# The low part of the normalised rows moved by 64 bytes in a two-part transformer kernel

## The chip, the cores and the metric

The kernel runs on one core of one Trainium2 chip. The metric is device time in microseconds (us) of one execution; lower is better. The engines are PE (TensorE; "PEld" are its weight loads), DVE (VectorE), ACT (ScalarE), POOL (GpSimd) and SP (SyncE), each with its own queue of instructions. A core has one SBUF of 128 partitions, in which all operands of the products lie.

## The reference

Two transformer parts run one after the other on a sequence of 256 rows of 1024 float32 numbers. The first has two layers, the second two. Cut to what the change touches:

```
h = rms_norm(x, g_mix[l]);  proj = h @ w_in[l]            # 1024 x 10052, split over four branches
x = x + merged @ w_merge[l]
h2 = rms_norm(x, g_ffn[l])
x = x + (silu(causal_dwconv(h2 @ w_ffn_gate[l])) * (h2 @ w_ffn_up[l])) @ w_ffn_down[l]
...
h = rmsnorm(x, norm_mix[layer]);  proj = h @ w_in          # second part: compressed and dilated attention
x = x + mix @ w_out
x = x + swiglu(rmsnorm(x, norm_ffn[layer]), ffn_w_up[layer], ffn_w_down[layer])
```

All weights are float32, and the result is to be close to a float32 computation.

## The kernel before

**Split products.** TensorE works in fp32r, a shortened float32. So every float32 operand is split into a high part (the value rounded to fp32r) and a low part (value minus high part), and each product is made in three passes by `three_passes`: high x high (L469), high x low (L470), low x high (L471). In the trace, a name pair as `psum<-hT,whi` gives the streamed operand first and then the one that is loaded as a block of weights.

**Weights.** They come in 277 units of up to 128x2048 numbers (8192 bytes a partition). SP loads a unit into one of three slots of `raw`; ACT makes the high part in one of four slots of `whi` (L437); DVE, or POOL for some, makes the low part in one of three slots of `wlo` (L445); PE multiplies. SP may refill a slot of `raw` once its low part is made.

**Rows.** The normalised rows, turned so that the 1024 features lie on the partitions, are `hT[0]` (high) and `hT[1]` (low), each of 8 x 256 numbers a partition. In the column form (`columns_product`, L486, and others) a block of the weights is loaded and the rows are streamed, 256 columns at a time: pass L470 streams `hT[1]` past a block of `whi`. In the row form (`psum<-whi,hT`) a block of the rows is loaded and the weights are streamed, 256, 512 or 68 columns at a time: pass L471 has a block of `hT[1]` loaded. `hT` is written by `whole_high` (L615, ACT) and `whole_low` (L623, DVE), and at the end of each mixing part by L1440 and L1710, L2161 and L2354, L2581 and L2632. The first units after each normalisation do not use `hT`: they use the not yet scaled rows in tiles of their own (`mixer_rows`, `ffn_rows`, `blocks_rows`, `dilated_rows`), which lie inside the large tile `work`, as do `branch` (the branches' outputs), `hidden` (of the feed-forward part) and `query_rows`.

**Order.** The kernel is a row of stages: for each layer a mixer or attention stage, then an output product (`add_rows_product`), then a feed-forward up stage (`ffn_up_stage`, 22 column units) and a down product (11 row units). The order of instructions on each engine is written out by hand. In `ffn_up_stage` DVE's queue holds, for each pair of units, the product of gate and value (`work` of L965) and after it the low parts of the next units (L445).

**Where tiles lie.** `sb` places tiles one behind the other, each start rounded up to 32 bytes: `x` (8192 bytes a partition), `h_place` (16896), `raw` (24576), `whi` (32768), `wlo` (24576), then `cst` (3816, rounded to 3840), `par` (3584), `g_head` (2048), `g_kidx` (512), `b_gl` (192), `rot` (384), `stat` (640) and `work`. `hT` is laid over `h_place` with a lead of `LEAD_ROWS` numbers:

```
PHASE = 512 // 4
LEAD_ROWS = PHASE - 16
h_place = sb("h_place", [P, 2 * KT * S + PHASE])
...
hT_both = over("hT", at_h, LEAD_ROWS, [2, KT, S])
hT = [hT_both[:, i] for i in range(2)]
```

Here P = 128, KT = 8, S = 256, and numbers are of 4 bytes. `over` only names an address; it costs no instruction. The tiles laid over `work` for rows begin at multiples of 32 numbers from its start.

Of the kernel before, what the change touches and what calls it, by code (L numbers as in the profile page):

```python
# [30 lines left out]
S = 256  # L31
TT = S // P
KT = D // P
# [200 lines left out]
def two_part_transformer(nc, a, consts, onehots, out):  # L234
    ctx = ExitStack()
    with ctx:
# [11 lines left out]
        LEAD_ROWS = PHASE - 16  # L248
# [18 lines left out]
        at_h, at_work = place["h_place"], place["work"]  # L267

        def over(name, base, start, shape, dt=F32R):

            return nc.alloc_sbuf_tensor_at(name, [P] + shape, dt, offset=base + 4 * start)

        hT_both = over("hT", at_h, LEAD_ROWS, [2, KT, S])
        hT = [hT_both[:, i] for i in range(2)]

        ROWS = 32
        table_dram = nc.dram_tensor("table_dram", [QH, ROWS, SPAN + 1], F32, kind="Internal").ap()
# [2531 lines left out]
```

How the kernel before makes its waits and increments, by code:

```python
        def begin(eng):  # L395
            if stage[0]:
                eng.wait_ge(stage_done.sem, COMPUTE * stage[0])
# [1 line left out]
        def end(eng):  # L399
            eng.drain().then_inc(stage_done.sem, 1)
# [10 lines left out]
        def v_wait(n):  # L411
            nc.vector.wait_ge(vector_step.sem, n)
# [9 lines left out]
        def s_wait(n):  # L422
            nc.scalar.wait_ge(scalar_step.sem, n)
# [6 lines left out]
        def make_high(act, upto):  # L430
            while stream.high < min(upto, len(stream.units)):
                n = stream.high
                act.wait_ge(raw_landed[n % RAW_SLOTS], 16 * (n // RAW_SLOTS + 1))
                if n >= HIGH_SLOTS:
                    act.wait_ge(*stream.freed[n - HIGH_SLOTS])
                act.activation(part(whi, n, HIGH_SLOTS), part(raw, n, RAW_SLOTS), ACT.Copy).then_inc(high_made, 1)
                stream.high += 1
# [1 line left out]
        def make_low(eng, n):  # L440
            eng.wait_ge(high_made, n + 1)
            if n >= LOW_SLOTS:
                eng.wait_ge(*stream.freed[n - LOW_SLOTS])
            eng.tensor_tensor(part(wlo, n, LOW_SLOTS), part(raw, n, RAW_SLOTS),
                              part(whi, n, HIGH_SLOTS).bitcast(F32), ALU.subtract).then_inc(stream.low[n][0], 1)
# [10 lines left out]
        def take_unit(pe, n):  # L457
            pe.wait_ge(*stream.low[n])
            _, kt, _, _ = stream.units[n]
            return [part(b, n, k).rearrange("p (k c) -> p k c", k=kt) for b, k in ((whi, HIGH_SLOTS), (wlo, LOW_SLOTS))]
# [18 lines left out]
        def await_pair(pe):  # L480
            if handed_over:
                pe.wait_ge(*handed_over.pop(0))
```

## Time and profile before

| | us |
|---|---|
| median of 3 runs | 1803.96 |
| lowest and highest of them | 1802.8, 1810.31 |
| the profiled execution | 1812.33 |
| its span, first to last instruction | 1810.5 |
| PE busy / PEld busy in the span | 1741.8 / 1638.3 |
| DVE / ACT / POOL busy | 1226.3 / 933.3 / 125.9 |

The mean granted clock of TensorE over the span is 0.983. Matmuls are pipelined: each lasts longer than the distance from one start to the next, so busy time of PE says only that it was not idle; the pace is read from the starts in the timeline. A few matmuls are missing from the records.

### The profile page before, as it was taken

What the parts mean: (1) busy time and instruction counts of PE and PEld (TensorE: products, weight loads), DVE (VectorE), ACT (ScalarE), POOL (GpSimd) and SP (SyncE); (2) the same over time, 40 slices, a digit from 0 to 9 for tenths busy, and PEclk for the clock granted to TensorE, in tenths of its full rate; (3) what the DMA queues carried; (4) which work ended last, traced back from release to release, by engine and by line L of the source; (5) the groups of instructions that cost most, each with busy time, mean ns of one, the idle gap of its engine ahead of it and who ended that gap; (6) DMA issues with size and microseconds to landing.
All of it is one profiled execution on the core that took longest, in us unless ns stands there. A gap on an engine that the chain in (4) does not pass through costs nothing.

```text
span 1810.5 us, 31727 instructions
## 1 busy us (share of the span) xinstructions
PE 1741.8 (96%) x13416; PEld 1638.3 (90%) x13416; DVE 1226.3 (68%) x1927; ACT 933.3 (52%) x1291; POOL 125.9 (7%) x35
## 2 busy tenths in 40 slices
PE   7989999999999999999999998889999999999998
PEld 6989999899989999999999898769998899889986
DVE  6985856787749868466877566877554656655553
ACT  5445655554445546654644355655443655654442
POOL 2610200000004603000000000000000000000000
PEclk9899999999999999999999989999999999999999
DMA  7684545555564554546455555324556576445562
GB/s 231 182 209 138 185 139 188 165 161 186 209 199 150 175 170 129 186 157 208 147 186 187 190 153 154 118 70 140 187 188 221 165 209 161 129 126 178 183 224 70
DMA packets 248636, 305.75 MB, mean 169 GB/s; under 512 B 9266, under 2 KB 223630, under 8 KB 248495
## 3 DMA queue, kind: packets, MB, share of 16 engines
q1 hardware_dynamic: 235959, 289.66, 49.9%
q10 hardware_dynamic: 12536, 14.06, 4.1%
q8 instruction: 106, 1.74, 0.4%
q14 instruction: 35, 0.29, 0.1%
HBM read 299.51 MB, written 4.19 MB: 168 GB/s over the span
## 4 chain that ended last, share of the span: by engine, by line
PE 59%; DVE 21%; DMA 8%; ACT 5%; issue 5%; DVEq 1%; ACTq 0%; SPq 0%
PE psum L469 18%; PE psum L471 17%; PE psum L470 17%; DVE wlo L445 7%; DMA raw<-in_w_ffn_gate 4%; DVE psum L1478 3%; DMA raw<-in_w_in 1%; ACT whi L437 1%; DMA raw<-in_w_ffn_down 1%; DVE work L965 1%; DVE work L1610 1%; PE psum L2479 1%; DMA work<-in_a_w_v 1%; PE psum L2505 1%; DVE work L1608 1%
## 5 line engine op out<-in xcount | busy, mean ns | idle before, releaser
L437 ACT ACTIVATE whi<-raw 128x2048 fp32r<-128x2048 f32 (+2 forms) x277 | 526.9, 1904 | 556.2 <-PE psum L471 178.4
L445 DVE TENSOR_TENSOR wlo<-raw,whi 128x2048 fp32r<-128x2048 f32 x249 | 563.6, 2282 | 182.9 <-PE psum L471 146.0
L469 PE MATMUL psum<-hT,whi 128*128 128x256 f32 x2160 | 608.2, 282 | 13.6 <-DVE wlo L445 11.7
L470 PE MATMUL psum<-hT,whi 128*128 128x256 f32 x2160 | 602.5, 279 | 0.0
L471 PE MATMUL psum<-hT,wlo 128*128 128x256 f32 x2160 | 602.3, 279 | 0.0
L469 PEld LDWEIGHTS psum<-hT,whi 128*128 128x128 f32 x2160 | 409.6, 190 | 18.8 <-DVE wlo L445 16.3
L470 PEld LDWEIGHTS psum<-hT,whi 128*128 128x128 f32 x2160 | 407.4, 189 | 0.2
L471 PEld LDWEIGHTS psum<-hT,wlo 128*128 128x128 f32 x2160 | 407.1, 188 | 0.0
L445 POOL TENSOR_TENSOR wlo<-raw,whi 128x2048 fp32r<-128x2048 f32 (+1 forms) x28 | 124.6, 4455 | 580.7 <-ACT whi L437 404.7
L469 PE MATMUL psum<-whi,hT 128*128 128x256 f32 (+2 forms) x448 | 144.5, 323 | 1.1 <-issue 0.8
L471 PE MATMUL psum<-whi,hT 128*128 128x256 f32 (+2 forms) x448 | 143.2, 320 | 0.0
L470 PE MATMUL psum<-wlo,hT 128*128 128x256 f32 (+2 forms) x448 | 143.0, 319 | 0.0
L469 PE MATMUL psum<-whi,hidden 128*128 128x512 f32 x352 | 139.0, 395 | 1.8 <-DVE hidden L971 0.6
L471 PE MATMUL psum<-whi,hidden 128*128 128x512 f32 x352 | 137.7, 391 | 0.0
L470 PE MATMUL psum<-wlo,hidden 128*128 128x512 f32 x352 | 137.2, 390 | 0.0
L965 DVE TENSOR_TENSOR work<-work,psum 128x512 f32<-128x512 f32 x44 | 30.3, 688 | 140.2 <-ACT work L907 62.6
L469 PEld LDWEIGHTS psum<-whi,hT 128*128 128x128 f32 x448 | 88.8, 198 | 8.2 <-issue 3.4
L1478 DVE SCALAR_TENSOR_TENSOR psum<-work,par,psum 128x256 f32<-128x256 f32 x240 | 94.7, 484 | 0.1
L471 PEld LDWEIGHTS psum<-whi,hT 128*128 128x128 f32 x448 | 88.7, 198 | 5.6
L470 PEld LDWEIGHTS psum<-wlo,hT 128*128 128x128 f32 x448 | 88.7, 198 | 5.1
L469 PEld LDWEIGHTS psum<-whi,hidden 128*128 128x128 f32 x352 | 66.1, 188 | 16.9 <-issue 1.8
L471 PEld LDWEIGHTS psum<-whi,hidden 128*128 128x128 f32 x352 | 66.1, 188 | 15.3
(361 smaller groups left out, 2801.0 us busy)
## 6 DMA issues: line engine op xcount, KB each, us to landing
raw<-in_w_in SPq DMA_DIRECT2D x78, 1024.0 KB, 5.6
raw<-in_ffn_w_up SPq DMA_DIRECT2D x44, 1024.0 KB, 5.3
raw<-in_w_ffn_gate SPq DMA_DIRECT2D x22, 1024.0 KB, 5.4
raw<-in_w_ffn_up SPq DMA_DIRECT2D x22, 1024.0 KB, 6.1
raw<-in_w_ffn_down SPq DMA_DIRECT2D x22, 1024.0 KB, 5.0
raw<-in_ffn_w_down SPq DMA_DIRECT2D x22, 1024.0 KB, 5.1
raw<-in_b_w_q SPq DMA_DIRECT2D x12, 1024.0 KB, 6.2
raw<-in_a_w_in SPq DMA_DIRECT2D x10, 1024.0 KB, 5.4
```

The source lines that it names most:

```text
L437: act.activation(part(whi, n, HIGH_SLOTS), part(raw, n, RAW_SLOTS), ACT.Copy).then_inc(high_made, 1)
L445: eng.tensor_tensor(part(wlo, n, LOW_SLOTS), part(raw, n, RAW_SLOTS), part(whi, n, HIGH_SLOTS).bitcast(F32), ALU.subtract).then_inc(stream ...
L469: nc.tensor.matmul(dst, left[0], right[0], start=first, stop=False)
L470: nc.tensor.matmul(dst, left[0], right[1], start=False, stop=False)
L471: return nc.tensor.matmul(dst, left[1], right[0], start=False, stop=last)
L965: v_link(dve.tensor_tensor(prod[:, c % 2], cacc[:, c % 2], u, ALU.mult))
L1478: ins = dve.scalar_tensor_tensor(acc, glu[:, ct, k:k + S], tap, acc, ALU.mult, ALU.add)
L1608: ins = dve.tensor_scalar(score[:, t, 0:L], rel[t][:, h, :], w, None, ALU.mult)
L1610: ins = dve.scalar_tensor_tensor(score[:, t, 0:L], rel[t][:, h, :], w, score[:, t, 0:L], ALU.mult, ALU.add)
L2479: mm = nc.tensor.matmul(slot(e)[:, st * keys:(st + 1) * keys], d_q[j // 2 % 2][lo:lo + DH, st, j % 2, t * P:(t + 1) * P], d_k[lo:lo + DH, ...
L2505: mm = nc.tensor.matmul(b[DH * e:DH * e + DH, t * P:(t + 1) * P], d_v[:, st, kt, g * DH:(g + 1) * DH], turned_probs[s % 2][:, 768 * e + n ...
```

## The change

Before, the high and the low part of the normalised rows are one tile, the low part 8192 bytes behind the high one. After, they are two tiles, and the low part starts 16 numbers (64 bytes) later. Nothing else is altered: no instruction, no order, no wait, no other tile.

```
-        hT_both = over("hT", at_h, LEAD_ROWS, [2, KT, S])
-        hT = [hT_both[:, i] for i in range(2)]
+        hT = [over(f"hT{i}", at_h, LEAD_ROWS + i * (KT * S + 16), [KT, S]) for i in range(2)]
```

## Rows read from the trace of the kernel before

**Rows 1.** The page: busy times, shares of the last chain, costliest groups.

```profile
PE 1741.8 (96%) x13416; PEld 1638.3 (90%) x13416; DVE 1226.3 (68%) x1927; ACT 933.3 (52%) x1291; POOL 125.9 (7%) x35
...
PE 59%; DVE 21%; DMA 8%; ACT 5%; issue 5%; DVEq 1%; ACTq 0%; SPq 0%
PE psum L469 18%; PE psum L471 17%; PE psum L470 17%; DVE wlo L445 7%; DMA raw<-in_w_ffn_gate 4%; DVE psum L1478 3%; DMA raw<-in_w_in 1%; ACT whi L437 1%; DMA raw<-in_w_ffn_down 1%; DVE work L965 1%; DVE work L1610 1%; PE psum L2479 1%; DMA work<-in_a_w_v 1%; PE psum L2505 1%; DVE work L1608 1%
...
L437 ACT ACTIVATE whi<-raw 128x2048 fp32r<-128x2048 f32 (+2 forms) x277 | 526.9, 1904 | 556.2 <-PE psum L471 178.4
L445 DVE TENSOR_TENSOR wlo<-raw,whi 128x2048 fp32r<-128x2048 f32 x249 | 563.6, 2282 | 182.9 <-PE psum L471 146.0
```

**Rows 2.** Waits of PE, longest first: total us, times, longest.

```profile
PE psum L469 <- DVE wlo L445: 14.2, 18, 1.9
PE psum L1960 <- DVE work L2294: 8.4, 15, 1.4
```

**Rows 3.** Page group (busy us, mean ns), then tile hT (ns min/median/max).

```profile
L470 PE MATMUL psum<-hT,whi 128*128 128x256 f32 x2160 | 602.5, 279 | 0.0
...
L471 PE MATMUL psum<-whi,hT x448: 276/279/415, 41.5 to 1611.4; 128*128 128x256 f32 x98, 128*128 128x512 f32 x42, 128*128 128x68 f32 x10
...
L623 DVE SCALAR_TENSOR_TENSOR hT<-psum,par,hT x56: 474/476/486, 370.1 to 1633.3; 128x256 fp32r<-128x256 f32 x56
L623 DVE SCALAR_TENSOR_TENSOR hT<-psum,first_gain,hT x8: 474/474/483, 34.8 to 37.6; 128x256 fp32r<-128x256 f32 x8
```

**Rows 4.** Timeline of PE, third feed-forward part: start us, duration us, what.

```profile
1340.01 0.28 PE L469 MATMUL psum<-hT,whi 128*128 128x256 f32 x1
...
1346.37 0.28 PE L469 MATMUL psum<-hT,whi 128*128 128x256 f32 x1
```

**Rows 5.** Timeline of PE, first feed-forward part.

```profile
421.12 0.28 PE L469 MATMUL psum<-hT,whi 128*128 128x256 f32 x1
...
423.50 0.28 PE L469 MATMUL psum<-hT,whi 128*128 128x256 f32 x1
```

**Rows 6.** Windows of the up products: busy us by engine, granted clock, DMA share, GB/s.

```profile
393.00:487.00 94.00, 90.46 (x755) 88.09 (x755) 71.00 (x90) 40.72 (x34) 0.00 (x0) 1.00 0.56 180
1256.00:1375.00 119.00, 118.74 (x965) 116.70 (x964) 67.65 (x53) 51.58 (x43) 0.00 (x0) 1.00 0.57 189
1631.00:1752.00 121.00, 117.53 (x963) 114.03 (x962) 67.11 (x53) 50.14 (x43) 0.00 (x0) 1.00 0.54 180
```

**Rows 7.** Timeline of all engines behind a wait, fourth feed-forward part.

```profile
1666.60 0.38 PE L469 MATMUL psum<-hT,whi 128*128 128x256 f32 x1 [0.35 <-DVE wlo L445]
...
1667.06 0.28 PE L469 MATMUL psum<-hT,whi 128*128 128x256 f32 x1
1667.06 0.19 PEld L470 LDWEIGHTS psum<-hT,whi 128*128 128x128 f32 x1
...
1668.08 0.28 PE L469 MATMUL psum<-hT,whi 128*128 128x256 f32 x1
```

**Rows 8.** Groups in the window 1300 to 1350: count, busy us, mean ns, idle.

```profile
L469 PE MATMUL psum<-hT,whi 128*128 128x256 f32 x143 | 40.2, 281 | 0.0
L470 PE MATMUL psum<-hT,whi 128*128 128x256 f32 x142 | 39.9, 281 | 0.0
L471 PE MATMUL psum<-hT,wlo 128*128 128x256 f32 x142 | 39.9, 281 | 0.0
...
L469 PEld LDWEIGHTS psum<-hT,whi 128*128 128x128 f32 x142 | 27.3, 192 | 0.0
L471 PEld LDWEIGHTS psum<-hT,wlo 128*128 128x128 f32 x142 | 26.7, 188 | 0.0
L470 PEld LDWEIGHTS psum<-hT,whi 128*128 128x128 f32 x142 | 26.7, 188 | 0.0
```

**Rows 9.** Groups of PE in the window 1665 to 1746.

```profile
L470 PE MATMUL psum<-hT,whi 128*128 128x256 f32 x212 | 58.5, 276 | 0.0
L471 PE MATMUL psum<-hT,wlo 128*128 128x256 f32 x212 | 58.5, 276 | 0.0
```

**Rows 10.** Timeline of DVE in the fourth feed-forward part.

```profile
1663.25 0.69 DVE L965 TENSOR_TENSOR work<-work,psum 128x512 f32<-128x512 f32 x1 [5.42 <-issue]
1664.25 4.49 DVE L445 TENSOR_TENSOR wlo<-raw,whi 128x2048 fp32r<-128x2048 f32 x2 [0.31 <-DVE work L965]
```

## Prediction

> **What bounds the kernel now.** I read the shares of the page first, then the chain of waits, then PE's own waits, and only then single matmuls. PE is busy for 96% of the span and its weight loads for 90% [rows 1]; the three lines of the product helper (469, 470, 471) alone carry 52% of the chain that ended last, DVE 21% and DMA 8% [rows 1]. PE waits little: the longest kind of wait is 14.2 us for `wlo` units [rows 2]. So the pace at which one matmul follows the next is the price that matters, above all on `hT`, which the change moves: 2160 triples with `hT` streamed past 128x128 weight blocks, and 448 triples with `hT` as the block that is loaded [rows 3].
>
> That pace has two values in the trace. In the up products of the third feed-forward part, L469 starts at 1340.01 and, 18 triples later, at 1346.37: 6.36 / 18 = 0.3533 us a triple, 117.8 ns a matmul [rows 4]. In the first feed-forward part it starts at 421.12 and, 7 triples later, at 423.50: 0.340 us a triple, 113.3 ns a matmul [rows 5]. [...] What differs is what went before: the quick pace sets in where PE has just waited for a unit. At 1666.60 L469 follows a wait of 0.35 us, and the quick pace stands behind it, 1667.06 to 1668.08 for 3 triples [rows 7]. The slow pace runs on in a stretch of 50 us without one idle moment [rows 8].
>
> In that slow stretch all three matmuls last 281 ns, and one of the three weight loads, that of L469, takes 192 ns where its two neighbours take 188 [rows 8]. In the other stretch the matmuls of L470 and L471 last 276 ns [rows 9]. Load and stream start together: the load of L470's block is recorded at 1667.06 with the matmul of L469 at 1667.06 [rows 7]. So two reads of SBUF run side by side, and how they meet seems to be worth 4.5 ns a matmul. [...]
>
> How much of the kernel is slow: over the whole span L470 on `hT` has a mean of 279 ns [rows 3]; between 276 and 281 that puts 3 in 5 of them at the slow pace (a few matmuls stretched by other causes make this somewhat too high).
>
> **The change part by part.** It removes no instruction, adds none, moves none in any queue, and changes no semaphore. Only where `hT[1]` lies is new. Does it do what it says? `x` (8192 bytes a partition), `h_place` (16896), `raw` (24576) and `whi` (32768) are multiples of 128 bytes, so every slot of `whi` and `wlo` begins in the phase of `h_place`. `hT[0]` begins 4 x 112 = 448 = 3 x 128 + 64 bytes behind it: 64 off, before and after. `hT[1]` begins 8192 further on before: 64 off too. After, it begins at element 112 + 2048 + 16 = 2176, byte 8704 = 68 x 128: in phase. It ends at element 4224, the end of `h_place`. The tiles in `work` (`mixer_rows`, `ffn_rows`, `branch`, `hidden`, `query_rows`) keep both parts 64 off: between `whi` and `work` lie `wlo` and 11200 bytes of small tiles, 87 x 128 + 64, and the tiles' own starts are multiples of 128.
>
> *Reads by TensorE.* In the column form L470 streams the low part while the block `wlo` for L471 is loaded; this pair of reads goes from 64 off to in phase, 2160 times. The other two pairs of the triple (high part against `whi`) stay as they are. In the row form L471's block is the low part, and it is loaded while L470 streams `wlo`: 448 times. So 2160 + 448 = 2608 matmuls in all have another pair of reads. The trace of before has no fp32r product with a part in phase, so the price is bounded by the nearest rows. Above: the step between the two paces, 4.5 ns, for each changed pair: 2608 x 4.5 = +11.7 us. Below: the same step as a gain, -11.7 us if it falls to the changed pair alone; if it takes the whole triple out of the slow pace, 2160 x 0.6 x 13.3 ns = -17.2 us. I take 0, the middle, for this reason: both paces appear at one and the same phase, and which of them holds follows from the last wait [rows 7, 8]. An offset of 64 bytes is thus not what chooses between them today. [...]
>
> [...]
>
> *Why a gain would not all arrive.* The third feed-forward part, nearly all slow, needs from 1256 to 1375 for its up products and shows PE busy for 118.74 of 119 us; the fourth, which is quick from 1665 on, needs from 1631 to 1752, with PE busy for 117.53 of 121 [rows 6]. It is the quicker matmuls that took the longer stretch: what they won went into waits for `wlo`, which DVE makes late behind `work` of L965 [rows 7, 10]. DMA moves 180 to 189 GB/s in both [rows 6]. So in the feed-forward parts, 88 of the units, a quicker triple buys next to nothing, and in the rest perhaps all of it. Halving 17.2 gives 9.
>
> *Writes and other readers.* Low parts are written by DVE: L623, 56 + 8 instructions of 474 to 486 ns [rows 3]; even if each went from one end of that spread to the other, 64 x 12 ns = 0.8 us, and most lies beside PE's products. `raw`, `whi`, `wlo` do not move, so the 2282 ns of a low unit on DVE and 1904 ns of a high one on ACT stay [rows 1]. The transfers do not touch `hT`.
>
> *The sum.* Profiled time 1812.3 us (span 1810.5 and 1.8 around it), plus 0, bounds -17 and +12.5. The three timed runs have their median at 1804.0, 8.4 below the profiled one, and reach from 1802.8 to 1810.3, so I put the forecast at the median: 1804 us. A spread of that size is what one would expect if waits fall a little differently and switch stretches between the two paces: 8 us are 600 triples at 13.3 ns.
>
> **The rivals.** *The second read collides (slower).* [...] It needs 9 / 2608 = 3.5 ns a pair to show; at 4.5 it gives 1804 + 12 = 1816 us, since PE stands at 96% and has no room to hide it.
>
> *The triple leaves the slow pace (faster).* The slow pace repeats exactly every triple, three equal pairs of offsets; with one pair different the pattern may not be able to hold itself. Then up to 17 us of PE time are freed, of which the waits above take back about half in the worst case: 1804 - 9 to 1804 - 17, 1791 in the middle. Against it: that the pattern is held by the phase at all is not shown; the quick pace came from waits.
>
> *It does what it says and nothing in TensorE minds (same).* This is the forecast, with the drift between the paces left in: 1798 to 1810. It covers also the case in which a gain is real and falls to the feed-forward parts only.
>
> **How the numbers follow.** Forecast, no change beyond 0.5%: 0.42. Faster by the broken pattern: 0.30. Slower by colliding reads: 0.28. About 0.5% (9 us) is what a measurement of this kernel tells from no change. The range takes in the middle of the faster case and the priced slower one with the spread of runs: 1790 to 1818; left out are a gain that arrives whole and a collision dearer than 5.4 ns a pair, together about 2 in 10. The forecast's own range is 1798 to 1810.
>
> **What would show it.** Right: both paces, 0.340 and 0.353 us a triple, again in the trace after, L470 on `hT` near 279 ns, and stretches on `ffn_rows` and `hidden` like those on `hT`. Slower: a third pace, 0.345 or more where it was 0.340, and the interval from L470 to L471 longer than the other two, in `hT` stretches alone. Faster: no stretch on `hT` at 0.353, while those on `ffn_rows` and `branch` still have it, and more waits for `wlo` on PE. Wrong altogether: instructions or waits that differ in number, or a granted clock that does.

## The result, and the profile after

Over 15 runs of each, the changed kernel takes 1811.61 us in the median (1801.71 to 1815.14), the kernel before 1805.18 us (1797.47 to 1810.55); the ratio is 1.0026, with a 95% interval of 1.0015 to 1.0037. So the change costs a quarter of a per cent, some 4.7 us (the two medians by themselves lie 6.4 us apart): less than the half per cent below which the prediction speaks of no change, but clear of the noise.

The page of the changed kernel. Its line numbers are one lower than before, so the three passes are now L468, L469 (the low part streamed) and L470:

```profile
PE 1747.1 (97%) x13416; PEld 1648.5 (91%) x13416; DVE 1224.0 (68%) x1927; ACT 932.2 (52%) x1291; POOL 124.2 (7%) x35
...
PE 76%; DVE 15%; DMA 4%; ACT 3%; issue 2%; DVEq 0%; ACTq 0%; SPq 0%
...
L436 ACT ACTIVATE whi<-raw 128x2048 fp32r<-128x2048 f32 (+2 forms) x277 | 526.7, 1904 | 548.7 <-PE psum L470 182.0
L444 DVE TENSOR_TENSOR wlo<-raw,whi 128x2048 fp32r<-128x2048 f32 x249 | 563.4, 2281 | 189.9 <-PE psum L470 155.8
...
L469 PE MATMUL psum<-hT,whi 128*128 128x256 f32 x2160 | 608.8, 282 | 0.0
```

Against [rows 1] and [rows 3], the counts are the same, ACT and DVE need the same for a unit (1904 and 2281 ns), and the chain that ended last has moved from DVE and DMA towards PE: PE has 59% of it before, 76% after. The matmul that streams the low part lasts 282 ns in the mean where it had 279. PE's waits, after (columns as in [rows 2]):

```profile
PE psum L468 <- DVE wlo L444: 6.5, 6, 1.7
PE psum L468 <- issue: 6.4, 9, 2.4
```

The wait for `wlo` has gone from 14.2 us in 18 pieces [rows 2] to 6.5 in 6. A second profile of each kernel, before and then after, says the same:

```profile
PE psum L469 <- DVE wlo L445: 13.3, 17, 1.9
...
PE psum L468 <- DVE wlo L444: 6.7, 7, 1.9
```

The timeline of PE in the first feed-forward part of the changed kernel, where [rows 5] has the quick pace:

```profile
420.95 0.28 PE L468 MATMUL psum<-hT,whi 128*128 128x256 f32 x1
...
424.53 0.28 PE L468 MATMUL psum<-hT,whi 128*128 128x256 f32 x1
```

Ten triples in 3.58 us: 0.358 us each, not 0.340. And in the third feed-forward part, where [rows 4] has 0.3533 (first every matmul of one triple, then the first matmul of some later ones):

```profile
1345.01 0.29 PE L468 MATMUL psum<-hT,whi 128*128 128x256 f32 x1
1345.13 0.28 PE L469 MATMUL psum<-hT,whi 128*128 128x256 f32 x1
1345.25 0.28 PE L470 MATMUL psum<-hT,wlo 128*128 128x256 f32 x1
1345.37 0.28 PE L468 MATMUL psum<-hT,whi 128*128 128x256 f32 x1
...
1346.08 0.29 PE L468 MATMUL psum<-hT,whi 128*128 128x256 f32 x1
...
1348.59 0.28 PE L468 MATMUL psum<-hT,whi 128*128 128x256 f32 x1
```

From 1345.01 to 1348.59 ten triples again take 3.58 us. Elsewhere after the change ten triples take 3.54 us, 0.354 each: L468 starts at 1299.77 and, ten triples later, at 1303.31.

```profile
1299.77 0.28 PE L468 MATMUL psum<-hT,whi 128*128 128x256 f32 x1
...
1303.31 0.28 PE L468 MATMUL psum<-hT,whi 128*128 128x256 f32 x1
```

To see the whole span at once I took every triple from the trace: the distance from one start of the first pass to the next one, three matmuls on, when it is under 400 ns (so that waits fall out, and stretches at the lower clock level, where a granted clock of 0.50 is shown, as from 1066 to 1070 us before, and a triple takes 640 ns or more). "Quick" is 342 ns or less. The placement is that of the high and the low part of `hT` in bytes modulo 512, counted from the weights. "Columns" is the column form, some 2040 to 2090 triples on `hT` and 690 on other tiles; "rows" is the row form with 256 columns streamed, some 265 triples. Means are in ns. This is my own count of the starts, not a view of the profile:

```
kernel                     high, low  hT, columns     hT, rows       other tiles, columns
                                      mean   quick    mean   quick   mean   quick
before                     448, 448   346.6  50%      349.6  28%     349.5  29%
before, second profile     448, 448   347.3  45%      351.1  17%     347.4  44%
after                      448, 0     354.9   0%      353.4   0%     347.6  43%
after, second profile      448, 0     355.1   0%      353.6   0%     347.3  45%
e1_both_in_phase           384, 384*  356.3   0%      356.0   0%     346.3  52%
e2_high_in_phase           384, 448   359.0   0%      354.3   0%     343.4  74%
e3_low_32_off              448, 480   356.6   0%      353.4   0%     348.5  36%
e4_low_moved_128           320, 448   353.2   0%      340.6  96%     342.5  80%
g3_low_moved_128_again     320, 448   352.9   0%      340.4  98%     345.5  58%
f1_change_on_low_moved     320, 0     356.7   0%      357.7   0%     349.0  32%
f2_both_moved_128          320, 320   350.9  19%      341.0  93%     349.8  26%
f3_low_weights_64_later    see there  354.7   0%      353.3   0%     353.4   0%
g1_half_loads_before       448, 448   349.0  33%      351.1  17%     348.5  36%
g2_half_loads_after        448, 0     354.2   0%      353.4   0%     347.5  43%
* 384 and 0 are 0 modulo 128 (in phase); 448 and 320 are 64 off; 480 is 96 off.
```

The quick pace has left `hT` altogether, in both forms, and stays on the tiles that the change does not touch. All three intervals of a triple have grown, not one: where a quick triple has 113.3 ns from each start to the next, the column form on `hT` after the change has 118.5, 119.6 and 116.8 in the mean. The longest is the one from the low part's stream to the next pass, by 1.1 ns over the first.

At one placement the share of quick triples is not the same in every execution. In the up products of the four feed-forward parts it is 82, 70, 0 and 80% in the first profile of the kernel before, and 22, 82, 0 and 48% in the second.

### The profile page after: what moved, and what is told of

The parts are those of the page before. It is cut to its first block, busy times and chain, and to the rows that moved or that the text cites. A ratio compares the mean times of both kernels' runs of the same rounds, so it can differ in the third digit from the quotient of the medians.

```text
span 1808.0 us, 31727 instructions
## 1 busy us (share of the span) xinstructions
PE 1747.1 (97%) x13416; PEld 1648.5 (91%) x13416; DVE 1224.0 (68%) x1927; ACT 932.2 (52%) x1291; POOL 124.2 (7%) x35
## 4 chain that ended last, share of the span: by engine, by line
PE 76%; DVE 15%; DMA 4%; ACT 3%; issue 2%; DVEq 0%; ACTq 0%; SPq 0%
PE psum L468 23%; PE psum L469 23%; PE psum L470 23%; DVE wlo L444 3%; DVE psum L1477 3%; DMA raw<-in_w_in 2%; PE psum L2478 1%; PE psum L2504 1%; DMA raw<-in_a_w_in 1%; PE psum L2490 1%; DMA raw<-in_b_w_q 1%; DVE work L2293 1%; DVE work L2277 1%; DVE work L1609 1%; ACT whi L436 1%
## 5 line engine op out<-in xcount | busy, mean ns | idle before, releaser
L436 ACT ACTIVATE whi<-raw 128x2048 fp32r<-128x2048 f32 (+2 forms) x277 | 526.7, 1904 | 548.7 <-PE psum L470 182.0
L444 DVE TENSOR_TENSOR wlo<-raw,whi 128x2048 fp32r<-128x2048 f32 x249 | 563.4, 2281 | 189.9 <-PE psum L470 155.8
L468 PE MATMUL psum<-hT,whi 128*128 128x256 f32 x2160 | 612.1, 283 | 6.9 <-DVE wlo L444 4.9
L469 PE MATMUL psum<-hT,whi 128*128 128x256 f32 x2160 | 608.8, 282 | 0.0
L470 PE MATMUL psum<-hT,wlo 128*128 128x256 f32 x2160 | 605.1, 280 | 0.0
L468 PEld LDWEIGHTS psum<-hT,whi 128*128 128x128 f32 x2160 | 406.7, 188 | 8.7 <-DVE wlo L444 5.9
L470 PEld LDWEIGHTS psum<-hT,wlo 128*128 128x128 f32 x2160 | 409.4, 190 | 0.0
L469 PEld LDWEIGHTS psum<-hT,whi 128*128 128x128 f32 x2160 | 407.5, 189 | 0.1
L468 PE MATMUL psum<-whi,hT 128*128 128x256 f32 (+2 forms) x448 | 143.0, 319 | 1.1 <-issue 0.8
L470 PE MATMUL psum<-whi,hT 128*128 128x256 f32 (+2 forms) x448 | 142.9, 319 | 0.0
L469 PE MATMUL psum<-wlo,hT 128*128 128x256 f32 (+2 forms) x448 | 142.7, 319 | 0.0
L468 PE MATMUL psum<-whi,hidden 128*128 128x512 f32 x352 | 138.6, 394 | 1.0 <-issue 1.0
L469 PE MATMUL psum<-wlo,hidden 128*128 128x512 f32 x352 | 137.7, 391 | 0.0
L470 PE MATMUL psum<-whi,hidden 128*128 128x512 f32 x352 | 137.3, 390 | 0.0
L468 PEld LDWEIGHTS psum<-whi,hT 128*128 128x128 f32 x448 | 87.4, 195 | 8.5 <-issue 3.4
L470 PEld LDWEIGHTS psum<-whi,hT 128*128 128x128 f32 x448 | 87.5, 195 | 5.5
L469 PEld LDWEIGHTS psum<-wlo,hT 128*128 128x128 f32 x448 | 87.2, 195 | 5.0
L468 PEld LDWEIGHTS psum<-whi,hidden 128*128 128x128 f32 x352 | 66.1, 188 | 15.9 <-issue 1.7
L470 PEld LDWEIGHTS psum<-whi,hidden 128*128 128x128 f32 x352 | 66.1, 188 | 15.1
```

The source lines that it names most:

```text
L436: act.activation(part(whi, n, HIGH_SLOTS), part(raw, n, RAW_SLOTS), ACT.Copy).then_inc(high_made, 1)
L444: eng.tensor_tensor(part(wlo, n, LOW_SLOTS), part(raw, n, RAW_SLOTS), part(whi, n, HIGH_SLOTS).bitcast(F32), ALU.subtract).then_inc(stream ...
L468: nc.tensor.matmul(dst, left[0], right[0], start=first, stop=False)
L469: nc.tensor.matmul(dst, left[0], right[1], start=False, stop=False)
L470: return nc.tensor.matmul(dst, left[1], right[0], start=False, stop=last)
```

## The experiments

**Which offset matters.** Four placements of `hT`. In the first three the weights stay where they are; in the fourth they move too. Each ratio below is to the kernel before, run alongside; for these four its median is 1809.35 us (28 runs), higher than the 1805.18 above, so that medians are to be compared within one group only. The lines that are altered:

```
e1  hT = [over(f"hT{i}", at_h, (96, 2144)[i], [KT, S]) for i in range(2)]
e2  hT = [over(f"hT{i}", at_h, (96, 2160)[i], [KT, S]) for i in range(2)]
e3  hT = [over(f"hT{i}", at_h, (112, 2168)[i], [KT, S]) for i in range(2)]
e4  hT = [over(f"hT{i}", at_h, (112, 2192)[i], [KT, S]) for i in range(2)]
    h_place = sb("h_place", [P, 2 * KT * S + PHASE + 32])
```

The starts are in numbers of 4 bytes. In the first both parts lie 384 bytes off the weights (modulo 512), which is 0 modulo 128: in phase, as the theories below use the word.

> Both parts of hT begin in the phase of the weights modulo 128 bytes (before: both 64 off; after the change: the low part alone in phase). Theory A, each pair of reads in phase costs on its own: all three pairs of a triple are in phase now, so no triple on hT takes 0.340 us, the usual one takes 0.357 or more, and the kernel is slower than the changed one, ratio to before 1.004 to 1.010. Theory B, only the mixture of two offsets in one triple spoils the quick pace: one offset for all three pairs, so stretches of 0.340 us come back, ratio 0.998 to 1.002. Theory C, the time is drift between runs and the offset is nothing: 0.340 and 0.353 as before, ratio 1.000.

Measured: ratio 1.0042 (1.0023 to 1.0061), median 1816.69. No quick triple on `hT`. Theory B (only a mixture spoils it) and theory C (the offset is nothing) fall: with one offset for both parts, but in phase, the quick pace is gone too.

> The mirror image of the change: the high part of hT in phase with the weights, the low part 64 bytes off. In the column form two pairs of the three are in phase, where the change has one. Theory A (each pair in phase costs on its own): worse than the changed kernel, triple 0.357 or more, ratio to before 1.003 to 1.008. Theory B (any mixture of offsets spoils the quick pace): no 0.340, triples of 0.353 to 0.357 as in the changed kernel, ratio 1.001 to 1.004.

Measured: 1.0071 (1.0050 to 1.0093), median 1821.76, and the dearest column triples of all, 359.0 ns. Two pairs in phase cost more than the change's one, as theory A has it; but three pairs (the run above: 356.3 ns, 1.0042) cost less than two, so the pairs do not simply add.

> The low part of hT 32 bytes later than before, so 96 bytes off the weights modulo 128, the high part 64 off as before: no pair is in phase, but the offsets in a triple are mixed. Theory A: no pair in phase, so the quick triple of 0.340 us stays, ratio 0.998 to 1.002. Theory B: mixed offsets, so no 0.340, ratio 1.001 to 1.004.

Measured: 1.0048 (1.0030 to 1.0066), median 1817.55, no quick triple on `hT` although no pair is in phase. So theory A by itself does not hold: a low part 96 off is no better than one in phase. Theory B had no 0.340 for this run either, but its ratio of 1.001 to 1.004 lies below the middle of what was measured.

> Control: the low part of hT is a tile of its own, 128 bytes later than before (h_place is 128 bytes larger, all tiles behind it lie 128 bytes later together), so every offset modulo 128 is that of before. Theories A and B: both paces, 0.340 and 0.353 us a triple, ratio 0.998 to 1.002. If a longer period than 128 bytes matters (512, say), the quick pace on hT is lost here too and the ratio is 1.001 to 1.004.

Measured: 0.9967 (0.9952 to 0.9982), median 1802.86. So this is not a neutral control. The expectation called every offset that of before. Modulo 128 that holds, but enlarging `h_place` moved the weights too, so that the high part is now at 320 instead of 448 modulo 512 and the low part is where it was. The quick pace is lost in the column form on `hT`, holds nearly throughout (96%) in its row form, and comes more often on the other tiles. The row form in this kernel, the first line and the last of six triples (0.340 us each):

```profile
89.83 0.28 PE L468 MATMUL psum<-whi,hT 128*128 128x256 f32 x1
...
91.87 0.28 PE L468 MATMUL psum<-whi,hT 128*128 128x256 f32 x1
```

and the same stretch of the changed kernel, five triples in 1.78 us, 0.356 each:

```profile
90.05 0.28 PE L468 MATMUL psum<-whi,hT 128*128 128x256 f32 x1
...
91.83 0.28 PE L468 MATMUL psum<-whi,hT 128*128 128x256 f32 x1
```

On `branch`, whose own place against the weights is the same in all these kernels, the faster kernel has eleven triples in 3.74 us (0.340):

```profile
317.94 0.28 PE L468 MATMUL psum<-branch,whi 128*128 128x256 f32 x1
...
321.68 0.28 PE L468 MATMUL psum<-branch,whi 128*128 128x256 f32 x1
```

where the kernel before has eleven in 3.89 us (0.354), with the same pace as on `hT` ahead of it:

```profile
317.96 0.28 PE L469 MATMUL psum<-branch,whi 128*128 128x256 f32 x1
...
321.85 0.28 PE L469 MATMUL psum<-branch,whi 128*128 128x256 f32 x1
```

So the pace on a tile that lies as before can differ between placements of `hT`. How is not shown: that an unequal offset between two tiles lets the pace be chosen anew would fit here, but not the two kernels below in which `hT` lies at other offsets than `branch` and the other tiles have only 26 and 32% quick triples.

**Is it the pair, and is 128 bytes the period.** Alongside these three the kernel before has 1809.64 us (23 runs).

```
f1  h_place as in e4;  hT = [over(f"hT{i}", at_h, (112, 2208)[i], [KT, S]) for i in range(2)]
f2  h_place as in e4;  hT as in the kernel before
f3  sb("gap0", [P, 16]) before wlo and sb("gap1", [P, 16]) behind it;  all else as before
```

> The change made on top of the control that came out faster (high part at 320 bytes modulo 512 from the weights, low part at 448): the low part goes 64 bytes further, to 0 modulo 128, the high part stays. Theory A, a pair in phase costs: the row form of the products on hT, wholly at 0.340 us a triple in the control, gets slower, and ratio to before 0.998 to 1.004, at least 0.003 above the control. Theory D, only the mixture in the last 512 bytes decides and every case is its own: the row form may keep 0.340 and the ratio stays at 0.997.

Measured: 1.0017 (0.9999 to 1.0035), median 1813.61, 0.005 above the kernel it was built on. The row form falls from 96% quick triples to none, 340.6 to 357.7 ns. The change does to this base what it does to the other: 64 bytes more on the low part take away what there is of the quick pace, and the kernel gets slower. That goes against theory D. It does not bring back theory A as a rule for every offset, which the low part 96 off had already refuted.

> h_place 128 bytes larger and nothing else: both parts of hT at 320 bytes modulo 512 from the weights, still 64 modulo 128. If only the offset modulo 128 counts, it is the kernel before: both paces on hT, ratio 0.998 to 1.002. If the different offset of the two parts made the control faster, the ratio here is again 1.000; if it was that the high part lies at 320 instead of 448, the ratio is 0.996 to 0.998.

Measured: 1.0001 (0.9981 to 1.0020), median 1810.78. Both paces are back in the column form (19% quick), the row form stays at 93% quick. Among the placements tried, the column form has quick triples only where both parts have the same offset and that offset is 64 off; the row form is quick nearly throughout where the high part is at 320 and the low part is 64 off. A shift by 128 bytes is thus not neutral for the pace, though the time is the same.

> hT as before, but the tile of the low weights lies 64 bytes later (with 64 more bytes behind it, so that work lies 128 bytes later), so that in every product, on hT and on all other tiles, L469's stream (the low part) runs beside the load of a low block at the same offset modulo 128: the pair that the change puts in phase, made by the other partner. Theory A (relative offset of the pair): no 0.340 in the column form on hT, branch, ffn_rows and query_rows alike, ratio 1.003 to 1.010. Theory E (the address of hT itself): hT as before, ratio 1.000.

The pass that streams the low part is L472 in this kernel, not the L469 of the expectation: two lines more stand ahead of the helper. Measured: 1.0077 (1.0052 to 1.0102), median 1825.06. With `hT` untouched and the low weights moved instead, there is no quick triple in any product of the kernel. On `branch`, eleven triples take from 325.00 to 328.88, 0.353 us each:

```profile
325.00 0.28 PE L471 MATMUL psum<-branch,whi 128*128 128x256 f32 x1
...
328.88 0.28 PE L471 MATMUL psum<-branch,whi 128*128 128x256 f32 x1
```

The wide products of `hidden`, which the change never touched, are also slower: five triples from 1390.22 to 1393.73, 0.702 us each, against six from 1389.27 to 1393.38 in the kernel before, 0.685. The first fence is this kernel, the second the kernel before:

```profile
1390.22 0.40 PE L471 MATMUL psum<-whi,hidden 128*128 128x512 f32 x1
...
1393.73 0.40 PE L471 MATMUL psum<-whi,hidden 128*128 128x512 f32 x1
```

```profile
1389.27 0.39 PE L469 MATMUL psum<-whi,hidden 128*128 128x512 f32 x1
...
1393.38 0.39 PE L469 MATMUL psum<-whi,hidden 128*128 128x512 f32 x1
```

Over 352 such triples 17 ns are 6 us. So theory E falls: with `hT` where it was, moving its partner takes the quick pace away as well. On `hT` this is clean, since only its distance to `wlo` is new; the tiles in `work` also lie 128 bytes further from `whi`, so for them the 64 bytes are not the only thing altered. That the distance between the two decides, and not the address of each, is the simplest reading of both moves; no run moved `hT` and all weights together by 64 bytes, so it is not shown apart.

**Second profiles.** The share of quick triples differs between executions of one kernel (82 and 22% in the first feed-forward part before), so a single one can mislead; here is another execution of each.

> The kernel before once more, for a second profile: on hT both 0.340 and 0.353 us again, in shares that may differ from the first profile by some hundred triples, since the waits fall differently.

> The changed kernel once more, for a second profile: triples on hT of 0.348 to 0.363 us and none of 0.340; the share of 0.340 on the other tiles may differ from the first profile.

Measured, one execution of each: 1808.90 us (span 1807.1) and 1807.27 us (span 1805.5). The counts of the table repeat: quick triples on `hT` in the column form 50% and 45% before, none and none after; on the other tiles the share in the kernel before went from 29% to 44%. The single executions do not repeat the order of the medians: both pairs have the changed kernel ahead, by 2.5 us (1812.33 and 1809.82) and by 1.6. Such a single pair says nothing on 0.26%; the timed runs decide.

**Where the lost time hides.** If the supply of weights hides part of the loss, a kernel with a faster supply should show it. The two kernels here are the one before and the changed one, with half of each unit loaded; what they compute is therefore not the reference's result.

```
+ some = kt if n < 12 or kt < 8 else kt // 2
  sp.dma_start(part(raw, n, RAW_SLOTS).rearrange("p (k c) -> p k c", k=kt)[:, 0:some, :],
               src.rearrange("(k p) c -> p k c", p=P)[:, 0:some, :])  # ... as before
```

> The kernel before, but each weight unit in column form from the 13th on is loaded by half only (the first four of its eight row blocks); the other half of the slot keeps the numbers of an older unit, so the result is not the reference's. TensorE's work is the same and the supply has room. Theory F (the quick triples on hT come from waits for units, and a slower triple is mostly paid out of such waits): PE waits for wlo less than in the kernel before, the share of 0.340 on hT falls below a third in the feed-forward parts, and the time falls by 0.2 to 1%.

> The same halved loads in the changed kernel. Theory F: with no supply waits both kernels run the slow triples, 0.353 before against a mean of about 0.356 after, so this one is slower than its partner by 2160 x 2.5 ns to 2160 x 4 ns = 5 to 9 us, about as far apart as with whole loads. Theory G (the quick pace on hT is independent of waits, and the waits for units hid the loss of it): the partner keeps half its triples at 0.340, and this one is slower by 15 to 17 us.

Measured, against the same runs of the kernel before (median 1810.28, 12 runs): 0.9882 (0.9857 to 0.9907), median 1789.17, for the first; 0.9931 (0.9908 to 0.9953), median 1798.78, for the second. They are 0.0049 x 1810 = 9 us apart, where the whole loads give 4.7; with six runs of each the 9 us are uncertain by about 5 (95%), so that "more than with whole loads" is likely but not clear of noise. In the first, PE waits less for `wlo`:

```profile
PE psum L469 <- DVE wlo L445: 4.7, 5, 1.9
```

and the quick share on `hT` is down from 45 to 50% to 33%. In the up products of the four feed-forward parts it is 100, 0, 0 and 0%, a quarter in all, as theory F has it. The first of these parts shows more. PE waits for `wlo` once, for 1.2 us ahead of the matmul at 376.00, and then every triple is quick; of this 256 triples in 87.04 us, 0.340 each:

```profile
380.20 0.28 PE L469 MATMUL psum<-hT,whi 128*128 128x256 f32 x1
...
467.24 0.28 PE L469 MATMUL psum<-hT,whi 128*128 128x256 f32 x1
```

The second part also has one wait for `wlo`, of 1.0 us, and is slow throughout. So a wait was followed by either pace, and in these two parts neither needed more waits to go on. Theory F is right in kind (fewer waits, fewer quick triples, 5 to 9 us between the two) and off in what it took for that: the kernel still has a third of its quick triples, and the time fell by 1.2%, more than its 1%. The 15 to 17 us of theory G lie outside what was measured.

One thing else differs between the two profiled executions. In the first mixing part the changed one waits twice for ScalarE, the other for neither of these:

```profile
PE psum L1120 <- ACT work L1376: 3.8, 1, 3.8
PE psum L468 <- ACT work L1245: 3.7, 1, 3.7
```

Waits of this kind come and go between kernels and between executions of one kernel (the second is also in the kernel with the high part in phase and in the change on the moved base). They are no waits for the weights' low parts, and 7.5 of the 12.2 us between these two spans are theirs. What sets them is not shown, so it is open how much of a ratio they make.

**A faster placement, run again.**

> The control that came out faster (high part at 320, low part at 448 bytes modulo 512 from the weights), once more, since it was picked from seven placements: if it is real the ratio to before is 0.995 to 0.999 and the row form on hT is again at 0.340 throughout; if it was luck, 0.999 to 1.002.

Measured: 0.9956 (0.9939 to 0.9973), median 1802.65; the row form on `hT` is 98% quick. The gain over the kernel before repeats.

## Why the prediction was right, and where its reasons failed

**The forecast** was no change within 0.5%, 1804 us, with a range of 1790 to 1818. The ratio of 1.0026 lies within it and the median of 1811.61 in the range; the forecast's own range of 1798 to 1810 does not reach that median. Of the 7.6 us between 1804 and 1811.61, 1.2 are a shift of the kernel before (1804.0 in three runs, 1805.2 in fifteen) and 6.4 lie between the two medians. The number was right in part by luck: the reason for a price of nothing failed, the pace lost more than the prediction's upper bound allowed, and waits that had little to do with that reason covered most of it.

**That the change does what it says** held: the counts and the cost of a unit on ACT and DVE are those of before.

**The step that failed** is the reason given for the value 0: that "an offset of 64 bytes is thus not what chooses between them", since both paces appear at one offset (and at one granted clock, 1.00 in the windows of both [rows 6]). In these runs what came before could decide between the two paces only where the placement showed both. On `hT` in the column form that is 64 off with equal offsets, [rows 4, 5] (45 to 50% quick) and the kernel with both parts moved (19%); with the low part in phase there was no quick triple, whatever waits came (0% in both profiles and in the halved loads). Nor does the last wait alone decide, as the prediction has it: with the halved loads the wait of 1.2 us was followed by the quick pace, the one of 1.0 us by the slow one. So the term put at 0 for the reads of TensorE was in truth a loss of 17.6 us in PE's pace. One assumption under it was weak as well: the 128 bytes, by which the prediction calls offsets equal. No row had shown them, and the row form on `hT`, with 17 to 28% quick triples at 448 and 93% with both parts at 320, shows that the full period is longer.

**The size of the price.** The bound of +11.7 us took one step of 4.5 ns for each of 2608 pairs. From the trace: leaving out waits (only distances under 130 ns from one start to the next, my own sums), the column form on `hT` has 6367 intervals of together 735.8 us before, 115.6 ns each, and 6415 of 758.8 us after, 118.3 ns each. Over the 6480 matmuls that is 17.6 us, or 8.1 ns for each of 2160 changed pairs, where the bound had 4.5: it is the whole triple that loses the quick pace, not one pair in it. (The prediction had the same step for a whole triple, 13.3 ns, as a possible gain of 17.2 us; it did not consider it as a loss. It took 3 in 5 of the triples for slow, where the starts show one half.) Against the slow pace itself the pair in phase costs little: 354.9 against 353.3 ns a triple.

**Where the 17.6 us went.** The intervals over 130 ns (waits, the slow first matmuls behind them, as the 0.38 us at 1666.60 [rows 7] beside 0.28, stretches at the granted clock of 0.50) are 113 with 50.4 us before and 65 with 32.5 us after. Undisturbed intervals grew by 23.0 us (48 more of them, at 0.118, are 5.7 of that), the disturbed ones shrank by 17.9, net 5.1 us. Most of the shrinking is in waits for `wlo`: 16 intervals with 16.1 us before, 5 with 6.2 after. Another 7.4 us are intervals at the full clock without a recorded wait, part of them right behind one: 68 with 15.6 us before, 38 with 8.2 after. The second pair of profiles gives 786.4 and 787.0 us in all, net 0.6. Both nets hold one wait for ScalarE that is none for weights (`work` of L1377, L1376 after): it went from 5.6 to 6.6 us in the first pair, from 5.6 to 2.3 in the second. Without it the nets are about 4.1 and 3.9 us, beside the timed 4.7.

```profile
PE psum L1121 <- ACT work L1377: 5.6, 1, 5.6
...
PE psum L1120 <- ACT work L1376: 6.6, 1, 6.6
...
PE psum L1120 <- ACT work L1376: 2.3, 1, 2.3
```

(The first line is in both profiles of the kernel before, the other two are in the first and the second after.) These nets are of the column form on `hT` alone; in the rest of the span the executions after were shorter by 7.6 and 2.2 us, which is why both pairs had the changed kernel ahead. The agreement with 4.7 is thus support and no proof. The prediction had the mechanism, "what they won went into waits for `wlo`" [rows 6, 7, 10], but used it for the gain alone; for the loss it wrote that PE "stands at 96% and has no room to hide it". PE had 14.2 us of waits for `wlo` [rows 2], with slow matmuls behind some of them, and about half of both went. The halved loads point the same way, within their noise: there the triples explain 1.75 ns x 6480 = 11 us, and 9 arrive.

**The rivals.** The colliding read, 1816 us, named the right sign and two of the right marks: no 0.340, and triples slower than 0.353 (0.358 over ten of them), on `hT` alone. Its third mark, a longer interval from the low part's stream to the next pass, is there by 1.1 ns over the next longest. Its condition was a price above 3.5 ns a pair: the pace lost 8.1 ns for each changed pair in the column form, but of the kernel's time only 4.7 us / 2608 = 1.8 ns arrived. That the mixture itself spoils the pattern was listed as a way to get faster; mixtures do matter (the low part 96 off, with column triples of 356.6 ns, and the high part at 320, with 353.2, neither with a quick one), but what they spoiled was the quick pace, not the slow one.

**How the two reads meet.** Placements 32 to 128 bytes apart move the pace of a triple on `hT` in the mean between 340 and 359 ns, and moving either partner does it. What in the hardware makes the difference, no run here shows; that two reads collide, or that a mixture breaks a pattern, was the author's guess.

**What stays open.** Why three pairs in phase cost less than two; why 96 off is as bad as 0; what the full period is. That it is longer than 128 bytes for the pace is shown by the row form on `hT`: 17 to 28% quick at 448, 93% or more with both parts, or the high one alone, at 320. Open too is what the pace of `hT` is worth in the kernel's time beyond the one change: with both parts moved the column form is slower than before (350.9 against 347 ns) at the same time, and in the fastest placement it is slower still (353). For that fastest one the trace gives most of the account. In whole intervals, waits included, its column form on `hT` takes 787.0 and 784.2 us in its two profiles, against 786.2 and 786.4 before: the slower triples are paid out of waits once more, 6.1 and 5.6 us for `wlo` in place of 14.2 and 13.3. The gain is in the rest: 1.4 to 2.0 us in the 256-column row form of `hT`, less 1.0 in its 512-column one, 1.7 to 4.9 on the column form of other tiles and 2.2 to 2.7 on their row form. First profile against first and second against second, these and the column form on `hT` make some 7 us each time; 6 and 8 were measured.

## What to carry to other kernels

A matmul's pace can hang on where its streamed operand lies against the block of weights that is loaded beside it: here the column form on `hT` went from 346.6 ns a triple to 356.6 and 354.9 with the low part 32 and 64 bytes further on, and the row form from 349.6 to 341.0 with both parts moved by 128 bytes. Read it from starts in the timeline, since PE's busy share (96 to 97% in all of these) does not show it. A pace that comes and goes at fixed addresses is not thereby free of the addresses (45 to 50% quick at one placement, none at another): ask which paces a placement allows, and then what chooses among them. And a loss can be covered by the same waits that would have eaten a gain: here 17.6 us of pace became 4.7 us of time. An engine that is busy for 96% of the span can still have such room.

## What the hardware showed that I had not expected

The pace goes on like a state. With both parts at 448 it ran unchanged across units and tiles: 0.353 us a triple for 287 triples on end in the third feed-forward part of the kernel before, 0.340 for 256 on end in the first part of the halved loads. In the kernel before every switch from one to the other lies where an interval of 160 ns or more stands between, or where one kind of product gives way to another (from the row form to the column form of `hT`, for one, with no interval longer than 0.12 us). Moving one tile by 64 bytes against the other took the 0.340 from `hT` (from 45 to 50% quick to none in the column form), and moving the low weights by 64 took it from every product; the wide products of `hidden` went from 0.685 to 0.702 us a triple. A shift by a full 128 bytes changed the share of quick triples in the row form from 17 to 28% to 93%.
